# Retention, folded down phases, first round and mixer side work in another order

## The chip, the cores and the metric

The kernel runs on one core of one Trainium2 chip. The metric is the device time of one execution in microseconds (us). Engines are named as in the profile: PE is TensorE, DVE is VectorE, ACT is ScalarE, POOL is GpSimd, and SP issues the loads.

## What is computed

Two transformer-like blocks follow each other, each of two layers, on 256 tokens of 1024 features, all in float32. The first block also carries 256 context tokens.

```python
for l in range(DEPTH):                      # first block
    x = half_ffn(x, m_lat, 0)               # t + 0.5*gate*swiglu(modulate(rmsnorm(t)))
    ctx = half_ffn(ctx, m_ctx, 0)
    h_lat, h_ctx = modulate(rmsnorm(x)), modulate(rmsnorm(ctx))
    if mixer == 0: y_lat, y_ctx = fourier_layer(h_lat, h_ctx, four_w, four_b)
    else: y_lat, y_ctx = retention_layer(h_lat, h_ctx, w_in, w_out, decay, cos, sin, False)
    x = x + m_lat[5] * y_lat
    x = half_ffn(x, m_lat, 2)
for l in range(DEPTH):                      # second block
    x = x + 0.5 * swiglu(rmsnorm(x), ffn1_w_in[l], ffn1_w_out[l])
    hq, hf, hi, hg, aq, ak, av, ga, gb = split(rmsnorm(x) @ w_in[l])
    y_a = (rms(hgrn2_chunk_scan(q, 1 - f, v, log f)) * norm * silu(hg)) @ w_branch_a[l]
    y_b = dilated_window_attention(rope(rms(aq)), rope(rms(ak)), av) @ w_branch_b[l]
    x = x + (sigmoid(ga) * y_a + sigmoid(gb) * y_b) @ w_out[l]
    x = x + 0.5 * swiglu(rmsnorm(x), ffn2_w_in[l], ffn2_w_out[l])
```

The retention layer has four heads. For each head it projects q, k, v and g, turns q and k by a rope, forms scores with a decay mask in both directions, multiplies them with v, normalises the result over its 512 values, multiplies it with silu(g), and projects the four heads together through w_out.

## The kernel before, in words

**Units and rounds.** Every matrix product is a phase. A phase goes through its weight in units of 128 output columns, and four units, one for each of four slots, make a round. A slot owns a raw weight buffer, a part of `whi_all` and `wlo_all`, and one PSUM bank (0 to 3). Banks 4 to 7 serve all side work. SP loads a unit's weights of `ks` blocks (128x128 each) into `raw`. ACT casts them to the high part (`split_hi`, L1073), DVE subtracts to get the low part (`split_lo`, L1343), and both signal SP and PE. PE multiplies each block three times, whi by hi, whi by lo and wlo by hi (`block_mm`, L613 to L615). Where only 256 tokens are left, whi meets hi and lo side by side in one matmul of 512 columns, and wlo one of 256 (L608, L609, L611: the folded form). When the unit is done (`mm_done`), ACT or DVE take its result, and ACT and DVE split the slot's next weights, which then wait three slots for PE. All engines hold their own instruction list, written in the order in which the Python code issues it; between engines there are only semaphores. What stands earlier on an engine must be done earlier.

**`linear`** writes a phase for PE. It has a special first round where the input is not complete yet. With `across`, the first half of the blocks goes block by block over all four slots; without it, slot 0 waits block by block and slots 1 to 3 follow whole. `do_first` and `do_norm` make the first normalised input: root of the mean square, then eight chunks of which DVE writes `t_full` (L1518), ACT the high and DVE the low part (`xn_two`, L1507). In the very first norm, a weight split stands behind chunks 1, 3 and 5.

**Feed-forward.** `gu` phases make gate and up, POOL writes the product in two parts (`h_two`, L1930 and L1932), and a `dn` phase reads them, in two halves of 12 and 10 blocks. The first unit of the `dn` phase comes to the last block when POOL has hardly written it.

**Retention, head by head.** `ret_qk`, `ret_v`, the turning of the values (L829, read from `r_vf`, which ACT copies out), `ret_g`, the scores (L838), the masked scores `r_p` (DVE, L1647), the result (L844), ten matmuls that compute nothing (`fill`, L721), the turning of the normalised result `r_yn` (L852, after DVE's statistics and ACT's root), and DVE's product with the gate (`r_z`, L1667), which POOL splits into `z_two` (L1939, L1941). After four heads `ret_out` reads `z_two`.

**Mixer.** `mixer_order` lists the units of eight phases, and behind each unit side work that all engines read from the same list. Unit 16 is the first of `att_qk` (QK), 40 of `hi` (HI), 60 of `hg` (HG). The scan over tokens works in eight levels of four units each: `decay` behind the first unit and `totals` behind the second (DVE, L1782 to L1801), `pairs` and `keep` for half 0 behind the third and for half 1 behind the fourth. `pairs` are PE's pair scores (L996, banks 4 and 5), `keep` is DVE's copy_predicated into `g_a` (L1809). A bank of `pairs` can be written again when the copy before has read it. `rope` i turns two heads' q (i below 6) or k on DVE (L1719 to L1724); for k, PE first spreads the roots (`spread`, L894) into bank 6, which it shares with `turn`, the turning of values (L935) that ACT copies out (`w_f`, L1279). `hsum` are row sums in bank 7 (L889), `hroot` ACT's and DVE's root of them, `hspread` j its spread (L894) and product (L1823).

```python
        for i, u in enumerate((21, 25, 29, 31, 33, 37, 43, 49, 51, 53, 55, 57)):
            if i >= 6:
                put(u, "spread", i)
            put(u, "rope", i)
```

Of the kernel before, what the change touches and what calls it, by code (L numbers as in the profile page):

```python
# [23 lines left out]
P = 128  # L24
# [54 lines left out]
def build(nc, A, out, stop=None):  # L79
# [105 lines left out]
    def mixer_order():  # L185
# [76 lines left out]
    with ExitStack() as ctx:  # L262
# [337 lines left out]
        def _(pe):  # L600
# [29 lines left out]
            def linear(name, moving, T, ready=None, across=False):  # L630
# [3 lines left out]
                ks, start = ph["ks"], 0  # L634
# [3 lines left out]
                def one(it, first=False):  # L638
# [14 lines left out]
                    for s in range(SLOTS):  # L653
# [5 lines left out]
                        for k in range(ks):  # L659
                            if first and name == "ret_out" and s < 2:  # L660
                                pe.wait_ge(*ready(8 * s + k))
                            elif first and s == 0:
# [106 lines left out]
            def do_ffn(a):  # L769
                two = h2_two if a["mod"] is None else h_two  # L770
                moving, ready = normed(a["norm"], folded(a))
                for half in range(2):
                    linear(f"{a['tag']}gu{half}", moving, a["T"], ready if half == 0 else None,
                           a["T"] == 2 * SEQ and a["norm"]["n"] > 0)
                    q0 = gu_rounds(a["f"], half)
                    linear(f"{a['tag']}dn{half}", pair(two, a["T"], folded(a)), a["T"],
                           lambda k: [(h_done[k % 2], q0 + k // 2 + 2)])
# [34 lines left out]
            def do_retention(a):  # L812
                _, ready = normed(a["norm"])
                for h in range(RH):
                    def tok(s):
                        return SEQ if s < 2 else 512
                    linear(f"ret_qk{h}", lambda s, k: pair(xn_two, tok(s))(s, k), tok,
                           ready if h == 0 else None, True)
                    linear(f"ret_v{h}", pair(xn_two, 512), 512)

                    pe.wait_ge(rt["vf"], 4 * (h + 1))
                    for t in range(4):
                        if h:
                            if t < 2:
                                pe.wait_ge(rt["yn"], 2 * h)
                            else:
                                pe.wait_ge(rt["z"], 2 * h)
# [3 lines left out]
                    linear(f"ret_g{h}", pair(xn_two, SEQ), SEQ)  # L831

                    pe.wait_ge(rt["qk"], 2 * (h + 1))
# [7 lines left out]
                    pe.wait_ge(rt["p"], 4 * (h + 1))  # L841
                    for i in range(2):
                        for j in range(4):
                            mm = pe.matmul(bank[4 + i][:], r_p[:, j, i * P:(i + 1) * P], r_v[:, j, :],  # L844
# [1136 lines left out]
```

## Time and profile before

| what | value |
|---|---|
| median of three runs | 3415.88 us (3411.71 to 3420.25) |
| the profiled execution | 3413.48 us |
| its span, first to last instruction | 3411.7 us |
| granted TensorE clock, mean | 0.993 of 2.4 GHz |
| PE busy | 3312.6 us |
| DVE, ACT, POOL busy | 2301.8, 1275.3, 648.5 us |
| mean DMA rate | 149 GB/s |

The rows of the views name engine, source line, operation and what is written from what. Behind a group or an instruction, in brackets or behind the bar, stands the engine's idle time before it and whose work ended it. The granted clock is given as a share of 2.4 GHz, so 0.50 is 1.2 GHz.

### The profile page before, as it was taken

The numbers are of one execution on the slowest core, as the hardware profiler recorded it, in microseconds if no ns is written. First come the engines' busy times: TensorE is split into PE (matmuls) and PEld (weight loads), VectorE is DVE, ScalarE is ACT, GpSimd is POOL, SyncE is SP. The second block draws the span as 40 slices with busy tenths as digits, with TensorE's granted clock in tenths as the row PEclk, the third lists the DMA queues.
The fourth block names the chain that finished last, engine by engine and source line by source line (L and its number), as shares of the span: only waits on it lengthen the run. The fifth ranks groups of instructions, "written<-read, shape, count | busy, mean of one in ns | idle before, by whom it ended". The sixth has DMA issues, their size and how long they took to land.

```text
span 3411.7 us, 49602 instructions
## 1 busy us (share of the span) xinstructions
PE 3312.6 (97%) x19035; PEld 2879.9 (84%) x19035; DVE 2301.8 (67%) x2888; ACT 1275.3 (37%) x1702; POOL 648.5 (19%) x535
## 2 busy tenths in 40 slices
PE   7999999999999999999999999999999999999999
PEld 4888888888888888878888899999888889899887
DVE  3877857878686545447677657756767666765766
ACT  2322133212321233334445343365534444346443
POOL 2212322212220220003242220000323230000222
PEclk9999999999999999999999999999999999999999
DMA  5655514646364423335665653345665655333664
GB/s 195 203 162 169 154 54 146 191 145 191 111 190 150 119 73 105 93 99 158 188 175 170 174 162 112 112 121 153 180 179 163 188 165 148 111 118 108 185 190 142
DMA packets 862983, 507.68 MB, mean 149 GB/s; under 512 B 15060, under 2 KB 843024, under 8 KB 862800
## 3 DMA queue, kind: packets, MB, share of 16 engines
q1 hardware_dynamic: 862432, 503.74, 49.9%
q8 instruction: 130, 2.13, 0.2%
q0 software_dynamic: 368, 1.38, 0.1%
q14 instruction: 53, 0.43, 0.0%
HBM read 504.01 MB, written 1.05 MB: 148 GB/s over the span
## 4 chain that ended last, share of the span: by engine, by line
PE 87%; DVE 7%; ACT 3%; issue 2%; POOL 1%; SPq 0%; DMA 0%; POOLq 0%; DVEq 0%; ACTq 0%
PE bank L613 17%; PE bank L611 17%; PE bank L615 16%; PE bank L614 16%; PE bank L609 10%; PE bank L608 2%; DVE wlo_all L1343 1%; ACT whi_all L1073 1%; PE bank L996 1%; DVE t_full L1518 1%; PE bank L702 1%; PE bank L844 1%; PE bank L734 1%; POOL h_two L1932 1%; PE bank L894 0%
## 5 line engine op out<-in xcount | busy, mean ns | idle before, releaser
L1343 DVE TENSOR_TENSOR wlo_all<-raw,whi_all 128x1024 fp32r<-128x1024 f32 (+3 forms) x768 | 1018.5, 1328 | 664.1 <-ACT whi_all L1073 661.3
L1073 ACT CAST whi_all<-raw 128x1024 fp32r<-128x1024 f32 (+3 forms) x768 | 834.5, 1089 | 901.2 <-PE bank L615 565.3
L613 PE MATMUL bank<-xn_two,whi_all 128*128 128x256 f32 (+1 forms) x2848 | 971.9, 341 | 12.3 <-DVE xn_two L1507 9.2
L614 PE MATMUL bank<-xn_two,whi_all 128*128 128x256 f32 (+1 forms) x2848 | 948.0, 333 | 0.0
L615 PE MATMUL bank<-xn_two,wlo_all 128*128 128x256 f32 (+1 forms) x2848 | 947.7, 333 | 0.0
L613 PEld LDWEIGHTS bank<-xn_two,whi_all 128*128 128x128 f32 x2848 | 543.6, 191 | 70.5 <-DVE xn_two L1507 11.1
L615 PEld LDWEIGHTS bank<-xn_two,wlo_all 128*128 128x128 f32 x2848 | 542.7, 191 | 52.0
L614 PEld LDWEIGHTS bank<-xn_two,whi_all 128*128 128x128 f32 x2848 | 543.5, 191 | 50.3
L611 PE MATMUL bank<-xn_two,whi_all 128*128 128x512 f32 x1540 | 550.3, 396 | 0.0
L609 PE MATMUL bank<-xn_two,wlo_all 128*128 128x256 f32 x1760 | 459.5, 281 | 3.3 <-DVE xn_two L1507 0.9
L1930 POOL CAST h_two<-silu_g 128x256 f32 (+1 forms) x176 | 197.2, 1121 | 1392.7 <-DVE silu_g L1558 783.7
L609 PEld LDWEIGHTS bank<-xn_two,wlo_all 128*128 128x128 f32 x1760 | 331.7, 188 | 33.5 <-DVE xn_two L1504 11.1
L611 PEld LDWEIGHTS bank<-xn_two,whi_all 128*128 128x128 f32 x1540 | 289.2, 188 | 58.1
L611 PE MATMUL bank<-h_two,whi_all 128*128 128x512 f32 x800 | 284.7, 396 | 0.0
L609 PE MATMUL bank<-h_two,wlo_all 128*128 128x256 f32 x880 | 234.0, 281 | 10.1 <-POOL h_two L1932 10.1
L1932 POOL TENSOR_TENSOR h_two<-silu_g,h_two 128x256 f32 (+1 forms) x176 | 224.6, 1276 | 32.5 <-POOL h_two L1930 32.5
L613 PE MATMUL bank<-h_two,whi_all 128*128 128x512 f32 x528 | 206.2, 390 | 0.0
L615 PE MATMUL bank<-h_two,wlo_all 128*128 128x512 f32 x528 | 205.5, 389 | 0.0
L614 PE MATMUL bank<-h_two,whi_all 128*128 128x512 f32 x528 | 205.5, 389 | 0.0
L1353 DVE SCALAR_TENSOR_TENSOR ada_acc<-ada_w,sil_c,ada_acc 128x1024 f32<-128x1024 f32 x112 | 183.0, 1634 | 0.8
L609 PEld LDWEIGHTS bank<-h_two,wlo_all 128*128 128x128 f32 x880 | 165.9, 188 | 20.5 <-POOL h_two L1932 13.3
L1907 POOL TENSOR_TENSOR sumsq<-x 128x256 f32<-128x256 f32 (+1 forms) x12 | 13.0, 1087 | 874.0 <-DVE x L1530 794.5
(281 smaller groups left out, 3855.4 us busy)
## 6 DMA issues: line engine op xcount, KB each, us to landing
raw<-in_ffn_w_in SPq DMA_DIRECT2D x176, 512.0 KB, 3.8
raw<-in_w_in SPq DMA_DIRECT2D x168, 512.0 KB, 3.7
ada_w<-in_ada_w SPq DMA_DIRECT2D x128, 512.0 KB, 3.8
raw<-in_ffn_w_gate SPq DMA_DIRECT2D x88, 512.0 KB, 3.7
raw<-in_ffn_w_up SPq DMA_DIRECT2D x88, 512.0 KB, 3.8
raw<-in_ffn_w_down SPq DMA_DIRECT2D x32, 768.0 KB, 5.1
raw<-in_ret_w_in SPq DMA_DIRECT2D x48, 512.0 KB, 3.8
raw<-in_ffn_w_out SPq DMA_DIRECT2D x32, 768.0 KB, 5.1
```

The lines of the kernel that those rows point to most:

```text
L608: pe.matmul(both, whi[s][:, k, :], two, start=True, stop=False)
L609: mm = pe.matmul(o, wlo[s][:, k, :], hi, start=False, stop=False)
L611: mm = pe.matmul(both, whi[s][:, k, :], two, start=False, stop=(k == ks - 1))
L613: pe.matmul(o, whi[s][:, k, :], hi, start=(k == 0), stop=False)
L614: pe.matmul(o, whi[s][:, k, :], lo, start=False, stop=False)
L615: return pe.matmul(o, wlo[s][:, k, :], hi, start=False, stop=(k == ks - 1))
L702: mm = pe.matmul(bank[half][0:4, :], first_cs[:, j, k, :], ada_first[DC * j + k][:, half * 512:(half + 1) * 512], start=(j == 0 and k == 0 ...
L1073: act.copy(whi[s][:, 0:ks, :], raw[s][:, 0:ks, :]).then_inc(hi_done[s], 1)
L1343: tt(wlo[s][:, 0:ks, :], raw[s][:, 0:ks, :], whi[s][:, 0:ks, :].bitcast(F32), ALU.subtract).then_inc(lo_done[s], 1)
L1353: stt(ada_acc[0][:], w[:], sil_c[:, k, 0:1], ada_acc[0][:], ALU.mult, ALU.add).then_inc(ada_sum, 1)
L1930: pool.tensor_copy(hi[:, ds(2 * it + p, 1), 0:T], full).then_inc(h_rounded[p], 1)
L1932: tt(lo[:, ds(2 * it + p, 1), 0:T], full, hi[:, ds(2 * it + p, 1), 0:T].bitcast(F32), ALU.subtract).then_inc(h_done[p], 1)
```

## The change

Four places get another order. The amount of work stays the same, but for forty filling matmuls that go.

1. **First round.** ACT and DVE split the weights of all four slots before they take the root, and none between the chunks. ACT squares its chunk ahead of that. The first round is written `across`.
2. **Down phases on 256 tokens** (`last_late`): in the first round, slots 0 and 1 do all blocks but the last; then PE waits for the last block and does it for both.
3. **Retention.** The values are turned behind the first unit of `ret_g`, the scores come behind the third; the result of a head is turned behind the first unit of the next head's `ret_qk`, or of `ret_out` for the last head. `fill(10)` is gone. `ret_out` takes its first round in the slot order 0, 2, 1, 3. DVE's pieces move along through `behind`.
4. **Mixer.** The twelve ropes get other units; `hsum`, `hroot` and `hspread` come one unit later.

```diff
-        for i, u in enumerate((21, 25, 29, 31, 33, 37, 43, 49, 51, 53, 55, 57)):
+        for i, u in enumerate((23, 27, 31, 35, 39, 43, 47, 50, 51, 54, 55, 58)):
...
-        put(HG, "hsum", 0)
-        put(HG, "hroot", 0)
+        put(HG + 1, "hsum", 0)
+        put(HG + 1, "hroot", 0)
         for j in range(4):
-            put(HG + 2 + j, "hspread", j)
+            put(HG + 3 + j, "hspread", j)
...
+                    if first and last_late:
+                        for s in range(2):
+                            slot_ready(s, r)
+                            for k in range(ks - 1):
+                                if s == 0:
+                                    for w in ready(k):
+                                        pe.wait_ge(*w)
+                                block_mm(s, k, ks, tokens(s), *moving(s, k))
+                        for w in ready(ks - 1):
+                            pe.wait_ge(*w)
+                        for s in range(2):
+                            block_mm(s, ks - 1, ks, tokens(s), *moving(s, ks - 1)).then_inc(mm_done[s], 1)
...
-                           a["T"] == 2 * SEQ and a["norm"]["n"] > 0)
+                           a["T"] == 2 * SEQ)
...
-                    fill(10)
...
+                for h in range(RH):
...
+                        for s in range(SLOTS):
+                            slot_mm(f"ret_qk{h}", 0, s, pair(xn_two, tok(s)), tok(s))
+                            if s == 0:
+                                turn_result(h - 1)
+                    linear(f"ret_v{h}", pair(xn_two, 512), 512)
+                    for s in range(SLOTS):
+                        slot_mm(f"ret_g{h}", 0, s, short, SEQ)
+                        if s == 0:
+                            turn_values(h)
+                        if s == 2:
+                            scores(h)
...
+                for s in (0, 2, 1, 3):
+                    slot_mm("ret_out", 0, s, halves[s % 2], SEQ, lambda k: (rt["zlo"], (8 * (s % 2) + k) // 4 + 1))
+                    if s == 0:
+                        turn_result(RH - 1)
...
             def do_first(a):
-                split_hi(0, 0, DC)
+                take_squares(a)
+                for s in range(SLOTS):
+                    split_hi(s, 0, DC)
                 take_root(a)
...
             def do_first(a):
-                split_lo(0, 0, DC)
+                for s in range(SLOTS):
+                    split_lo(s, 0, DC)
                 take_root(a)
```

DVE in the very first norm, from the first weight split on. Before:

```order
L1343 TENSOR_TENSOR wlo_all_50<-raw0,whi_all_49 128x1024
L1482 RECIPROCAL rstd<-rstd 128x4
L1389 TENSOR_TENSOR mod<-bank5,vec 128x16 x2
L1393 SCALAR_TENSOR_TENSOR mod<-mod,vec 128x16
L1518 SCALAR_TENSOR_TENSOR t_full_56<-x_53,mod,bank7 128x256 x4
L1507 SCALAR_TENSOR_TENSOR xn_two_54<-t_full_56,mod,xn_two_54 128x256 x2
L1343 TENSOR_TENSOR wlo_all_50<-raw1,whi_all_49 128x1024
```

and now:

```order
L1384 TENSOR_TENSOR wlo_all_50<-raw0,whi_all_49 128x1024
L1384 TENSOR_TENSOR wlo_all_50<-raw1,whi_all_49 128x1024
L1384 TENSOR_TENSOR wlo_all_50<-raw2,whi_all_49 128x1024
L1384 TENSOR_TENSOR wlo_all_50<-raw3,whi_all_49 128x1024
L1526 RECIPROCAL rstd<-rstd 128x4
L1430 TENSOR_TENSOR mod<-bank5,vec 128x16 x2
L1434 SCALAR_TENSOR_TENSOR mod<-mod,vec 128x16
L1562 SCALAR_TENSOR_TENSOR t_full_56<-x_53,mod,bank7 128x256 x4
```

The splits of slots 1 to 3 moved from between the chunks to ahead of the root's reciprocal.

PE at the turn from one head to the next. L838 are the scores, L844 (now L885) the result, L721 the filling matmuls, L852 (now L859) the turning. Before:

```order
L613 MATMUL bank<-xn_two,whi_all 128x256
L614 MATMUL bank<-xn_two,whi_all 128x256
L615 MATMUL bank<-xn_two,wlo_all 128x256
L838 MATMUL bank<-r_q,r_k 128x256 x8
L844 MATMUL bank<-r_v,r_p 128x512 x8
L721 MATMUL bank<-ident 128x128 x10
L852 MATMUL bank<-ident,r_yn 128x128 x8
L613 MATMUL bank<-xn_two,whi_all 128x256
```

and now, at the result, and 24 matmuls of the next head later at the turning:

```order
L613 MATMUL bank<-xn_two,whi_all 128x256
L614 MATMUL bank<-xn_two,whi_all 128x256
L615 MATMUL bank<-xn_two,wlo_all 128x256
L885 MATMUL bank<-r_v,r_p 128x512 x8
L613 MATMUL bank<-xn_two,whi_all 128x256
```

```order
L613 MATMUL bank<-xn_two,whi_all 128x256
L614 MATMUL bank<-xn_two,whi_all 128x256
L615 MATMUL bank<-xn_two,wlo_all 128x256
L859 MATMUL bank<-ident,r_yn 128x128 x8
L613 MATMUL bank<-xn_two,whi_all 128x256
```

The scores went one unit up, the turning one unit down, and nothing is left between result and next unit.

DVE in a mixer level (the fourth of eight), from the end of its totals to its last copy. L1719 to L1724 (now L1767 to L1772) are a rope, L1809 (now L1857) the kept pairs. Before:

```order
L1699 RECIPROCAL square<-square 128x24
L1719 TENSOR_TENSOR a_s_116<-a_qk_114,rope2_119 64x512 x2
L1722 TENSOR_TENSOR a_qk_114<-a_qk_114,rope2_119 128x512
L1724 TENSOR_TENSOR a_qk_114<-a_qk_114,a_s_116 128x512
L1343 TENSOR_TENSOR wlo_all_50<-raw2,whi_all_49 128x1024
L1809 COPY_PREDICATED g_a0_110<-hmask_120,bank4 128x2x2x128
L1809 COPY_PREDICATED g_a1_111<-hmask_120,bank5 128x2x2x128
L1343 TENSOR_TENSOR wlo_all_50<-raw3,whi_all_49 128x1024
L1809 COPY_PREDICATED g_a2_112<-hmask_120,bank4 128x2x2x128
L1809 COPY_PREDICATED g_a3_113<-hmask_120,bank5 128x2x2x128
```

and now:

```order
L1747 RECIPROCAL square<-square 128x24
L1384 TENSOR_TENSOR wlo_all_50<-raw2,whi_all_49 128x1024
L1857 COPY_PREDICATED g_a0_110<-hmask_120,bank4 128x2x2x128
L1857 COPY_PREDICATED g_a1_111<-hmask_120,bank5 128x2x2x128
L1384 TENSOR_TENSOR wlo_all_50<-raw3,whi_all_49 128x1024
L1857 COPY_PREDICATED g_a2_112<-hmask_120,bank4 128x2x2x128
L1857 COPY_PREDICATED g_a3_113<-hmask_120,bank5 128x2x2x128
L1767 TENSOR_TENSOR a_s_116<-a_qk_114,rope2_119 64x512 x2
L1770 TENSOR_TENSOR a_qk_114<-a_qk_114,rope2_119 128x512
L1772 TENSOR_TENSOR a_qk_114<-a_qk_114,a_s_116 128x512
```

The rope went from ahead of the level's copies to behind them.

## Rows read from the trace of the kernel before

**Rows 1.** The page: busy time of the engines, and the ended-last chain by engine.

```profile
PE 3312.6 (97%) x19035; PEld 2879.9 (84%) x19035; DVE 2301.8 (67%) x2888; ACT 1275.3 (37%) x1702; POOL 648.5 (19%) x535
...
PE 87%; DVE 7%; ACT 3%; issue 2%; POOL 1%; SPq 0%; DMA 0%; POOLq 0%; DVEq 0%; ACTq 0%
```

**Rows 2.** Who waited for whom, PE: total us, times, longest us.

```profile
PE bank L996 <- DVE g_a L1809: 20.7, 14, 2.1
PE bank L609 <- POOL h_two L1932: 10.1, 10, 1.7
...
PE bank L852 <- DVE r_yn L1660: 3.7, 4, 0.9
PE bank L894 <- ACT w_f L1279: 3.6, 2, 1.8
PE bank L889 <- ACT w_f L1279: 3.2, 2, 1.6
PE bank L894 <- DVE g_d L1823: 2.9, 2, 1.4
PE bank L829 <- ACT r_vf L1198: 2.7, 4, 0.7
...
PE bank L844 <- DVE r_p L1647: 2.4, 4, 0.6
```

**Rows 3.** Timeline, first round, PE and ACT: start, us, instruction, idle before.

```profile
51.66 0.47 PE L613 MATMUL bank<-xn_two,whi_all 128*128 128x512 f32 x1 [1.35 <-DVE xn_two L1507]
...
70.33 0.39 PE L613 MATMUL bank<-xn_two,whi_all 128*128 128x512 f32 x1
...
83.93 0.39 PE L613 MATMUL bank<-xn_two,whi_all 128*128 128x512 f32 x1
...
86.17 1.05 ACT L1073 CAST whi_all<-raw 128x1024 fp32r<-128x1024 f32 x1 [3.91 <-PE bank L615]
```

**Rows 4.** Windows, 56 to 69 us: busy of each engine, PEclk, DMA share, GB/s.

```profile
56.00:69.00 13.00, 8.64 (x18) 5.08 (x18) 10.17 (x22) 7.17 (x12) 0.00 (x0) 0.50 0.31 92
```

**Rows 5.** Timeline of DVE, two chunks of the first norm.

```profile
54.18 0.87 DVE L1507 SCALAR_TENSOR_TENSOR xn_two<-t_full,mod,xn_two 128x256 fp32r<-128x256 f32 x2
...
55.76 0.87 DVE L1507 SCALAR_TENSOR_TENSOR xn_two<-t_full,mod,xn_two 128x256 fp32r<-128x256 f32 x2
```

**Rows 6.** Windows, 43 to 44 us, and ACT's root.

```profile
43.00:44.00 1.00, 1.00 (x10) 1.00 (x10) 0.00 (x0) 0.00 (x0) 0.00 (x0) 1.00 0.80 214
...
44.89 0.26 ACT L1105 ACTIVATE rstd<-bank,eps 128x4 f32<-128x4 f32 x1 [4.42 <-PE bank L734]
```

**Rows 7.** Timeline of retention: end of head 0, PE; end of head 3, DVE, POOL.

```profile
1323.84 7.13 PE L844 MATMUL bank<-r_v,r_p 128*128 128x512 f32 x16 [0.61 <-DVE r_p L1647]
1330.81 2.40 PE L721 MATMUL bank<-ident 128*128 128x128 f32 x20
1334.14 1.09 PE L852 MATMUL bank<-ident,r_yn 128*128 128x128 f32 x8 [0.93 <-DVE r_yn L1660]
...
1539.02 1.29 DVE L1667 TENSOR_TENSOR r_z<-bank,r_g 128x512 f32<-128x512 f32 x2 [0.85 <-PE bank L852]
...
1540.38 1.04 POOL L1939 CAST z_two<-r_z 128x1024 fp32r<-128x1024 f32 x1 [64.38 <-DVE r_z L1667]
1541.50 2.40 POOL L1941 TENSOR_TENSOR z_two<-r_z,z_two 128x1024 fp32r<-128x1024 f32 x1
```

**Rows 8.** Timeline of PE, first unit of a second down phase.

```profile
1755.57 0.39 PE L609 MATMUL bank<-h_two,wlo_all 128*128 128x256 f32 x1 [1.66 <-POOL h_two L1932]
```

**Rows 9.** Timeline of DVE, mixer of layer 0: a copy and a rope.

```profile
2116.34 0.73 DVE L1809 COPY_PREDICATED g_a<-hmask,bank 128x512 f32<-128x512 int32 x1 [0.79 <-PE bank L996]
2117.09 1.40 DVE L1719 TENSOR_TENSOR a_s<-a_qk,rope 64x512 f32<-64x512 f32 x2
2118.53 0.69 DVE L1722 TENSOR_TENSOR a_qk<-a_qk,rope 128x512 f32<-128x512 f32 x1
2119.26 0.69 DVE L1724 TENSOR_TENSOR a_qk<-a_qk,a_s 128x512 f32<-128x512 f32 x1
```

**Rows 10.** Windows, two levels of the mixer of layer 1, second half to second half.

```profile
2899.39:2918.51 19.12, 17.05 (x143) 16.83 (x143) 14.72 (x18) 7.93 (x14) 0.00 (x0) 1.00 0.38 111
2918.51:2939.00 20.49, 18.59 (x137) 18.08 (x137) 17.37 (x21) 6.37 (x12) 0.00 (x0) 0.92 0.35 103
```

More of the change, by code:

```diff
@@ L628, in ada_reduce, with slot_mm, linear @@
                     mm.then_inc(ada_cols, 1)
-            def linear(name, moving, T, ready=None, across=False):
+            def slot_mm(name, it, s, moving, T, ready=None):
                 ph = phases[name]
-                ks, start = ph["ks"], 0
+                slot_ready(s, it + ph["first"])
+                for k in range(ph["ks"]):
+                    if ready is not None:
+                        pe.wait_ge(*ready(k))
+                    mm = block_mm(s, k, ph["ks"], T, *moving(s, k))
+                mm.then_inc(mm_done[s], 1)
+            def linear(name, moving, T, ready=None, across=False, last_late=False, start=0):
+                ph = phases[name]
+                ks = ph["ks"]
                 tokens = T if callable(T) else (lambda s: T)
@@ L652, in one @@
                         return
-                    for s in range(SLOTS):
+                    if first and last_late:
[10 more added lines that the diff above has]
+                            block_mm(s, ks - 1, ks, tokens(s), *moving(s, ks - 1)).then_inc(mm_done[s], 1)
+                    for s in range(2 if first and last_late else 0, SLOTS):
                         slot_ready(s, r)
@@ L813, in do_retention, with turn_values @@
                 _, ready = normed(a["norm"])
[L814 to L819, printed above, removed]
+                def turn_values(h):
                     pe.wait_ge(rt["vf"], 4 * (h + 1))
@@ L830, in do_retention, with scores @@
                         mm.then_inc(rt["vt"], 1)
-                    linear(f"ret_g{h}", pair(xn_two, SEQ), SEQ)
+                def scores(h):
                     pe.wait_ge(rt["qk"], 2 * (h + 1))
@@ L840, in do_retention, with turn_result @@
                         mm.then_inc(rt["s"], 1)
[L841 to L844, printed above, removed]
-                                           start=(j == 0), stop=(j == 3))
-                        mm.then_inc(rt["y"], 1)
-                    fill(10)
+                def turn_result(h):
                     pe.wait_ge(rt["yn"], 2 * (h + 1))
@@ L1117, in do_norm @@
                 if a["n"]:
+                    take_squares(a)
                     take_root(a)
@@ L1415, in body @@
                             split_lo(s, r + 1, ahead)
+                        if behind is not None:
+                            behind(it, s)
                         if ends and SLOTS * r + s in ends:
@@ L1604, in do_retention, with take_result @@
                 cos, sin = rope1[:, 0, :], rope1[:, 1, :]
+                def take_result(h):
+                    g3 = phases[f"ret_g{h}"]["first"] + 2
+                    for s in range(SLOTS):
+                        dve.wait_ge(bank_free[s], g3)
+                    for b in range(2):
+                        dve.wait_ge(rt["yt"], 2 * h + b + 1)
+                        tt(r_z[:, 2 * b:2 * b + 2, :], bank[6 + b][:].rearrange("p (e t) -> p e t", e=2),
+                           r_g[:, 2 * b:2 * b + 2, :], ALU.mult).then_inc(rt["z"], 1)
                 for h in range(RH):
@@ L1629, in rope @@
                         tt(dst[:, 1, 0:SEQ], r_t[:, 2, :], r_t[:, 3, :], ALU.add).then_inc(rt["qk"], 1)
-                    stream(f"ret_qk{h}", rope, True)
+                    stream(f"ret_qk{h}", rope, True, behind=lambda it, s: h and s == 0 and take_result(h - 1))
                     dve.wait_ge(rt["expo"], h + 1)
@@ L1661, in do_retention @@
                             ALU.mult).then_inc(rt["yn"], 1)
-                    g3 = phases[f"ret_g{h}"]["first"] + 2
-                    for s in range(SLOTS):
-                        dve.wait_ge(bank_free[s], g3)
-                    for b in range(2):
-                        dve.wait_ge(rt["yt"], 2 * h + b + 1)
-                        tt(r_z[:, 2 * b:2 * b + 2, :], bank[6 + b][:].rearrange("p (e t) -> p e t", e=2),
-                           r_g[:, 2 * b:2 * b + 2, :], ALU.mult).then_inc(rt["z"], 1)
                 def add(it, s, r):
```

57 lines of the change are left out of this document (33 added, 24 removed).

## The prediction

> **What bounds the kernel now.** I read the page first. TensorE (PE) is busy 3312.6 us of a span of 3411.7 us, and it makes 87% of the chain that ended last [rows 1]; no weight load is waited for after the first 50 us. So the sum is made on PE alone: a change can only take away PE's idle time, PE's slow time, or matmuls that compute nothing. Anything another engine does is hidden until PE waits for it. The second view, who waited for whom on PE, prices the idle time [rows 2]. The third, the timeline and the windows around each wait, tells what is behind it, and how fast PE's clock was. PE's matmuls of 512 columns follow each other every 0.2267 us in steady work (60 of them from 70.33 to 83.93 us) [rows 3]; I use 0.227 us for 512 columns and half of it for 256.
>
> **The change part by part.**
>
> *First round.* The first round of linear work starts at 51.66 us, and its fourth slot is done when ACT takes it at 86.17 us [rows 3]: 34.5 us for 96 matmuls that need 96 x 0.2267 = 21.8 us. Two things cost the rest. DVE and ACT put a weight split between every two normalised chunks, so the last chunk comes only at 66.9 us, while slots 1 to 3 wait behind slot 0; and in the 13 us from 56 to 69 the granted clock is 0.50, the lower level of 1.2 GHz, after PE was mostly idle [rows 4]. The change does the four splits before the norm and lets all slots use a chunk as it comes. A chunk then costs DVE two pieces of 0.79 us, 1.58 us in all (54.18 to 55.76 us) [rows 5], while its 12 matmuls take PE 12 x 0.2267 = 2.72 us. PE is slower than its supplier, so it starts at about the same 51.7 us and never stops: end at 51.7 + 21.8 = 73.4 us, **12.8 us** earlier. The cost is that ACT and DVE now wait for three more weight blocks ahead of the root. The loads run until about 44 us (the DMA share is still 0.80 from 43 to 44), and ACT takes the root at 44.89 us [rows 6]. The last cast is then done by about 45, a table load and the root follow, and the reciprocal ends some 0.3 us after PE wants it. I take 12.5 us. Bounds: 6 us, if the clock still falls for 13 us with PE busy (half of 13), and 12.8 us.
>
> *Retention, four heads.* Now PE waits 2.7 us (4 times) for the values to be evacuated before it turns them and 2.4 us (4) for the scores [rows 2]. With one or two slots of the gate phase in between (24 matmuls x 0.113 = 2.7 us each) both waits are covered: **5.1 us**. Behind the result matmuls stand ten filling matmuls, in 20 records, that take from 1330.81 to about 1333.2, and a wait of 0.93 us; from 1330.97, the end of the results, it is 3.17 us until the turning starts at 1334.14 [rows 7]. The first slot of the next head, 2.9 us with its overlap, comes in that place, so 0.3 us stays: 2.9 us x 3 = **8.6 us** for three heads. For the fourth the cover is a slot of the output phase, 2.8 us. There the turned result is late next: DVE has to finish slot 0's residual and split first, then multiplies (1.29 us), and POOL needs 1.04 + 2.40 us for its two pieces [rows 7]. The result reaches z_lo some 6.2 us after the turning; slot 2 and half of slot 1 cover 4.2 us. PE waits 2.0 us where it now waits 0.4. The fourth head gives 3.17 - 0.4 - 1.6 = 1.2 us. Sum **14.9 us**; bounds 10 (each head's turn waits 1 us more) and 17.
>
> *Down phases.* Ten times PE stops before the last block of the first slot until POOL has written it, 10.1 us in all [rows 2], one of 1.66 us in each second half [rows 8] and so about 0.36 us in each first. Now slot 1's blocks but the last go ahead of it: at least nine blocks of 768 columns, 9 x 0.34 = 3.1 us, more than any wait. The first slot is free later by that much, but the next use of it comes two slots (7 us) on, and its residual and splits need about 5. **10.1 us**; bounds 8 and 10.1.
>
> *Mixer, two layers.* DVE decides when a level's second half of pair scores can start: it needs the first copy_predicated. A rope of four instructions, 1.40 + 0.69 + 0.69 with gaps, is 2.77 us (2117.09 to about 2119.86) [rows 9], and before it stands between the totals and that copy. It now stands behind the level's last copy. From a level's last copy to the next level's first, DVE has the rope 2.8, three splits 3.4, decays 2.3, totals 2.4 and the copy 0.7 = 11.6 us. By the time these have to be done PE has run from one second half to the next, 17.05 us [rows 10], less about 4.3 us from its start to the end of DVE's last copy (ACT's pieces 1.8, a split 1.14, two copies of 0.62 to 0.73 as in rows 9): 12.8 us. That leaves 1.2 us free. So the five waits of 1.30 to 2.07 us of a layer, 9.1 of 10.35 us, go, and those of 0.97 us (a reciprocal stands there) and 0.28 us stay: 2 x 9.1 = **18.2 us**. The row sums one unit later clear the copies of ACT: 2 x 1.6 = **3.2 us** [rows 2]. The third key spread no longer comes right behind turned values, 2 x 1.82 us [rows 2], but two key ropes are now in neighbouring units just before a turn that shares their bank; DVE is then some 0.9 us late for it: **1.8 us** net. The wait of 1.44 us a layer for the spreads of the hg root (L894 for g_d) [rows 2] is set by ACT's work of one fixed unit; it moves from the fourth spread to the third and stays. Sum of mixer waits **23.2 us**; bounds 15 (the pairing costs 4 us a layer) and 27.
>
> **Sum** 12.5 + 14.9 + 10.1 + 23.2 + 10.8 = **71.5 us**. The profiled execution took 3413.48 us with a span of 3411.7, 2.4 us under the median of 3415.88. From itself it gives 3342.0; I forecast the median, 3415.9 - 71.5 = **3344 us**, 2.1% less.
>
> The Trainium skill speaks against one part. "TensorE: Matmul & The Clock Gate", section "HAM oscillation", says that pauses between bursts throttle the array again and cost half of the throttled time. By that rule the filling matmuls that the change drops did a job, and the result would be the second rival's 3352 us rather than 3344; that half of the time is lost agrees with the 1.54 us of rows 10.
>
> **The rivals.**
> 1. *The clock's share does not come.* The lower level is granted at norms too, where no such wait stands, so the waits may not be what brings it. If the seven stay, the time is 3344 + 11 = 3355; if the first round also falls to it for its 13 us, 3361. For it: layer 1 has a wait of 1.94 without a low stretch. Against: no level behind a short wait has one. Chance 0.14.
> 2. *The head turns lose the clock.* Without the filling matmuls, the idle 0.3 to 2 us of four turns and the output phase bring one low stretch each: 5 x 1.54 = 8 us, 3352. Chance 0.08.
> 3. *DVE becomes the bound in the mixer.* If the 1.2 us of slack is not there (a POOL operation beside it, ropes in neighbouring units), each of 14 levels still waits 1 us, and the low clock with it: 3344 + 14 + 7 = 3365. For it: DVE is busy 17.37 of 20.49 us in a level with a second piece [rows 10]. Chance 0.08.
> 4. *It does less than it says in the down phases or the first round*, because another engine was late as well: half of 22.6 us, 3355. Chance 0.06.
> 5. *Slower than before.* The fills and the ordered waits keep TensorE at the upper level, and without them retention and the mixers run at 1.2 GHz for long. PE-bound work at the lower level loses half of its time, so 71.5 us are lost again when it lasts 143 us; over the four heads of 68 us it would be +136 us, 3480. The rows 4 show 13 us of it after a gappy stretch, never more. Chance 0.02.
>
> **How the numbers follow.** The forecast has 0.62. Rivals 1 to 4 have 0.36 together and lie between 3352 and 3365. The forecast's own bounds are about 3331 (the three low places at norms go too, the last head does not wait, the mixer gives 27) and 3358. The range is 3330 to 3363: it leaves out the end of rival 3, rival 5, and gains beyond the upper bounds. A measurement of this kernel tells about 0.3% (10 us) from no change. Only rival 5 is on the other side, and for within 0.3% most terms would have to fail at once: faster 0.97, same 0.01, slower 0.02.
>
> **What would show it.** In the profile after: the first round's fourth slot taken at about 73.7 us with clock 1.00 throughout; no wait of PE for h_two; no filling matmuls and no waits for r_vf and r_p in retention, about 0.3 us for r_yn three times, about 2 us for z_two once; PE's wait for g_a under 3 us in total instead of 20.7, none behind row sums, one of about 1.5 us for g_d in each layer; levels of 17 us at clock 1.00. PE's busy time should fall by about 9 us of fills, 11 us of slow clock and what the first round's slow matmuls were worth. Wrong would be: a wait for g_a near 14 us, low clock in levels without a wait, or a new wait for weights (wlo_all) after the paired key ropes.

## The result and the profile after

| | before | after |
|---|---|---|
| median, us | 3416.98 (4 runs, 3411.71 to 3420.25) | 3336.19 (4 runs, 3335.01 to 3337.18) |
| ratio | | 0.9765, 95% from 0.9748 to 0.9782 |
| profiled execution, us | 3413.48 | 3336.21 |
| its span, us | 3411.7 | 3334.4 |

The changed kernel is 2.35% faster. The forecast was 3344 us, the range 3330 to 3363: the time lies in the range, 8 us below the forecast. The gain is 79.7 us against the median of 3415.88 shown above, 80.8 us against that of four runs, and 77.3 us between the two profiled spans. The forecast gain was 71.5. The sums below are made on the two traces, so against 77.3.

The page of after, busy time and the chain by engine (before: [rows 1]):

```profile
PE 3281.3 (98%) x18955; PEld 2859.5 (86%) x18955; DVE 2294.6 (69%) x2888; ACT 1274.4 (38%) x1702; POOL 648.4 (19%) x535
...
PE 92%; DVE 4%; ACT 2%; issue 1%; SPq 0%; DMA 0%; POOL 0%; DVEq 0%; ACTq 0%
```

The 80 matmul records that are missing (19035 to 18955) are the forty filling matmuls, two records each. PE's idle time fell from 99.1 to 53.1 us, its busy time from 3312.6 to 3281.3. Who waited for whom on PE, after (line, total us, times, longest us; before: [rows 2]):

```profile
PE bank L1034 <- DVE g_a L1857: 3.1, 4, 1.3
PE bank L932 <- DVE g_d L1871: 2.9, 2, 1.4
...
PE bank L609 <- POOL z_two L1989: 1.5, 1, 1.5
PE bank L973 <- issue: 1.4, 2, 0.7
...
PE bank L859 <- DVE r_yn L1715: 1.3, 4, 0.4
```

L1034 is L996 of before: its wait for the kept pairs went from 20.7 us (14 times) to 3.1 (4). The waits for h_two, r_vf, r_p and both for w_f have no row any more. The wait for g_d is unchanged at 2.9, that for z_two grew from 0.4 to 1.5, and that at L973 (`turn`, the turning of values, L935 before) is new. The timeline of after, at the places that the prediction named (start, us, instruction, idle before):

```profile
44.16 1.04 ACT L1111 CAST whi_all<-raw 128x1024 fp32r<-128x1024 f32 x1 [1.87 <-DMA raw<-in_ffn_w_up]
46.52 0.26 ACT L1147 ACTIVATE rstd<-bank,eps 128x4 f32<-128x4 f32 x1
...
52.46 0.47 PE L613 MATMUL bank<-xn_two,whi_all 128*128 128x512 f32 x1 [1.35 <-DVE xn_two L1551]
74.54 1.05 ACT L1111 CAST whi_all<-raw 128x1024 fp32r<-128x1024 f32 x1 [1.19 <-PE bank L615]
1320.99 1.09 PE L859 MATMUL bank<-ident,r_yn 128*128 128x128 f32 x8 [0.30 <-DVE r_yn L1715]
1511.08 1.09 PE L859 MATMUL bank<-ident,r_yn 128*128 128x128 f32 x8 [0.39 <-DVE r_yn L1715]
1517.91 0.39 PE L609 MATMUL bank<-z_two,wlo_all 128*128 128x256 f32 x1 [1.54 <-POOL z_two L1989]
```

The first round runs from 52.46 to 74.54, 22.1 us instead of 34.5 [rows 3]. Windows of after: the stretch of [rows 4], then two levels of layer 0's mixer from one second half to the next (before, in layer 1: [rows 10]), then most of each mixer, then retention (bounds, length, busy us of PE, PEld, DVE, ACT, POOL, granted clock, DMA share, GB/s):

```profile
56.00:69.00 13.00, 13.00 (x59) 10.78 (x58) 7.54 (x18) 6.35 (x11) 0.00 (x0) 1.00 0.01 1
...
2056.55:2073.37 16.82, 16.82 (x145) 16.77 (x144) 14.67 (x17) 8.03 (x14) 0.00 (x0) 1.00 0.43 125
2090.13:2106.90 16.77, 16.77 (x138) 16.56 (x137) 14.58 (x16) 6.37 (x12) 0.00 (x0) 1.00 0.43 126
2000.00:2300.00 300.00, 294.41 (x2361) 289.00 (x2361) 211.13 (x264) 152.04 (x254) 0.00 (x0) 1.00 0.42 123
2780.00:3080.00 300.00, 294.42 (x2361) 289.00 (x2360) 210.78 (x263) 151.51 (x253) 0.00 (x0) 1.00 0.43 124
1240.00:1560.00 320.00, 314.65 (x1747) 265.86 (x1746) 179.42 (x288) 123.22 (x167) 34.57 (x26) 1.00 0.37 108
```

Levels of 19 to 20.5 us became levels of 16.8 us in which PE never stops, and both mixers run at clock 1.00. Layer 1's mixer before, taken for 300 us from 45 us behind its start (42 in after), had 2216 matmuls instead of 2361, at clock 0.98:

```profile
2840.00:3140.00 300.00, 282.90 (x2216) 276.22 (x2215) 202.59 (x250) 142.32 (x235) 0.00 (x0) 0.98 0.40 117
```

The first matmul that sums the squares of a norm (L754, L734 before) marks the stages. Four of its rows in after:

```profile
419.30 0.35 PE L754 MATMUL bank<-ones,sumsq 128*128 128x1 f32 x2 [0.42 <-ACT silu_g L1142]
1247.96 0.35 PE L754 MATMUL bank<-ones,sumsq 128*128 128x1 f32 x2 [0.42 <-ACT silu_g L1142]
1557.60 0.35 PE L754 MATMUL bank<-ones,sumsq 128*128 128x1 f32 x2 [0.74 <-ACT silu_g L1142]
1955.79 0.35 PE L754 MATMUL bank<-ones,sumsq 128*128 128x1 f32 x2 [0.65 <-ACT silu_g L1142]
```

Before they stood at 430.93, 1258.41, 1586.41 and 1988.26. A stage is the time from one of these markers to the next. With the other markers, the 77.3 us by which the span is shorter are made of:

| part | forecast, us | traces, us |
|---|---|---|
| start and first round | 12.5 | 11.6 (0.8 later start, 12.4 shorter) |
| from the first round to retention (419 to 1248) | 0 | -1.2 (the clock at the norms) |
| retention | 14.9 | 18.4 |
| down phases | 10.1 | 11.1 (3.7 + 5.0 + 2.5) |
| mixers and their clock | 23.2 + 10.8 | 37.4 (19.5 + 17.9) |
| sum | 71.5 | 77.3 |

### The profile page after: what moved, and what is told of

The parts are those of the page before. It is cut to its first block, busy times and chain, and to the rows that moved or that the text cites. A ratio compares the mean times of both kernels' runs of the same rounds, so it can differ in the third digit from the quotient of the medians.

```text
span 3334.4 us, 49439 instructions
## 1 busy us (share of the span) xinstructions
PE 3281.3 (98%) x18955; PEld 2859.5 (86%) x18955; DVE 2294.6 (69%) x2888; ACT 1274.4 (38%) x1702; POOL 648.4 (19%) x535
## 4 chain that ended last, share of the span: by engine, by line
PE 92%; DVE 4%; ACT 2%; issue 1%; SPq 0%; DMA 0%; POOL 0%; DVEq 0%; ACTq 0%
PE bank L613 18%; PE bank L611 18%; PE bank L615 18%; PE bank L614 18%; PE bank L609 10%; PE bank L608 2%; PE bank L1034 1%; DVE t_full L1562 1%; PE bank L722 1%; PE bank L885 1%; ACT whi_all L1111 1%; PE bank L754 1%; DVE wlo_all L1384 1%; PE bank L932 0%; PE bank L927 0%
## 5 line engine op out<-in xcount | busy, mean ns | idle before, releaser
L609 PEld LDWEIGHTS bank<-xn_two,wlo_all 128*128 128x128 f32 x1760 | 331.9, 189 | 33.2 <-DVE xn_two L1548 10.8
L611 PEld LDWEIGHTS bank<-h_two,whi_all 128*128 128x128 f32 x800 | 150.3, 188 | 32.8
```

Source lines behind the costliest of these rows:

```text
L609: mm = pe.matmul(o, wlo[s][:, k, :], hi, start=False, stop=False)
L611: mm = pe.matmul(both, whi[s][:, k, :], two, start=False, stop=(k == ks - 1))
```

## The experiments

**1 to 4. Each part undone alone.** In `undo_mixer` the two tables of the mixer are as before:

```
-for i, u in enumerate((23, 27, 31, 35, 39, 43, 47, 50, 51, 54, 55, 58)):
+for i, u in enumerate((21, 25, 29, 31, 33, 37, 43, 49, 51, 53, 55, 57)):
-put(HG + 1, "hsum", 0); put(HG + 1, "hroot", 0); put(HG + 3 + j, "hspread", j)
+put(HG, "hsum", 0); put(HG, "hroot", 0); put(HG + 2 + j, "hspread", j)
```

> The changed kernel with the mixer's side work in the old order; all else as changed. By the forecast's terms it loses 23.2 us of waits and 10.8 us of slow clock: 3336.2 + 34.0 = 3370. If every stop of PE costs about 0.2 us more than its recorded idle time (the restart of the matmul stream), 16 stops a time for both layers add 3 us: 3373. PE's wait for g_a is 20.7 us again and seven levels have a clock of 0.92. If the low clock depends on where PE stands and not on the waits, the number of such levels differs from seven, 1.54 us each.

Measured 3373.70 us (3373.01 to 3374.83), ratio 0.9877 [0.9861, 0.9894]: 37.5 us more than the change. Its waits, and a stretch of layer 1's mixer:

```profile
PE bank L1034 <- DVE g_a L1857: 20.7, 14, 2.1
...
PE bank L932 <- ACT w_f L1320: 3.6, 2, 1.8
PE bank L927 <- ACT w_f L1320: 3.2, 2, 1.6
PE bank L932 <- DVE g_d L1871: 2.9, 2, 1.4
```

```profile
2840.00:2930.00 90.00, 82.20 (x621) 80.92 (x620) 65.37 (x74) 28.83 (x52) 0.00 (x0) 0.92 0.36 105
```

All the waits of before are back, with nothing else of the change undone. The low clock is back too, in six places (a low place is one stretch at the lower level), though not the same ones: one in layer 0 and five in layer 1, where before had four and three. That gives the price of both by themselves. In the old order the stage of layer 0's mixer took 415.78 us with four low places (before) and 410.94 with one (`undo_mixer`), that of layer 1 414.16 with three and 417.48 with five. So a low place costs 1.6 to 1.7 us, and without any the two stages would take 409.3 and 409.2, which is 25.9 us more in all than the 396.29 each of after. That is the price of the waits; the other 11.4 of the 37.4 us are the clock's.

`undo_down` gives the first slot of the down phases its last block in its own turn again:

```
-..., last_late=folded(a))
+...)
```

> The changed kernel with slot 0 of the folded down phases waiting for its last block as before. Recorded idle alone: 10.1 us in ten waits, 3336.2 + 10.1 = 3346.3. Idle plus a restart of about 0.2 us each: 3348.6. If the two traces' difference of 12.4 us in these stages came from elsewhere, it is under 3345.

Measured 3347.63 us (3346.80 to 3349.69), ratio 0.9802 [0.9785, 0.9818]: 11.4 us more. One row is new against after:

```profile
PE bank L609 <- POOL h_two L1980: 10.1, 10, 1.7
```

Ten waits that the profile puts at 10.1 us cost 11.4 by the median. The stages of the two traces tell more: where neither has a low place, a stage with two down phases takes 196.11, 195.46 and 195.47 us instead of 193.62, 192.97 and 192.99. That is 2.49, 2.49 and 2.48 us for two waits that are recorded with 2.02 to 2.05, or 0.21 to 0.23 us a stop beyond its record.

`undo_first` puts the splits of slots 1 to 3 back between the chunks and lets slots 1 to 3 wait behind slot 0:

```
-for s in range(SLOTS):
-    split_hi(s, 0, DC)
+split_hi(0, 0, DC)
...
+if a["n"] == 0 and k in (1, 3, 5):
+    split_hi((k + 1) // 2, 0, DC)
...
-... a["T"] == 2 * SEQ)
+... a["T"] == 2 * SEQ and a["norm"]["n"] > 0)
```

(and the same for `split_lo` on DVE).

> The changed kernel with the first round as before (one split ahead, three between the chunks, slots 1 to 3 behind slot 0). Forecast's term: 3336.2 + 12.5 = 3348.7, with a clock of 0.50 for about 13 us. If half of the gain was the clock's alone and the clock stays up this time, about 3342.

Measured 3347.91 us (3347.02 to 3348.33), ratio 0.9801: 11.7 us more. The stretch of [rows 4] is again at the lower level of 1.2 GHz:

```profile
56.00:69.00 13.00, 8.79 (x18) 5.19 (x19) 9.94 (x21) 6.93 (x12) 0.00 (x0) 0.50 0.31 93
```

`undo_ret` has PE's and DVE's retention of before: the values are turned right behind the value phase, the scores are made behind the whole gate phase, ten filling matmuls stand behind the result, and it is turned before the next head. In words, the edit is:

```
-scores(h) in the gate phase's slot 2, turn_values(h) in its slot 0
-turn_result(h - 1) behind the next head's first slot
+turn_values(h) ahead of the gate phase, scores(h) behind all of it
+fill(10); turn_result(h) at the head's end
```

> The changed kernel with the whole retention layer in the old order, filling matmuls included. Forecast's term: 3336.2 + 14.9 = 3351.1. With a restart of about 0.2 us for each of eight to twelve stops: 3353. The rival that the fills held the clock up: it would gain clock back and be under 3349.

Measured 3354.25 us (3353.33 to 3354.74), ratio 0.9819 [0.9803, 0.9836]: 18.1 us more.

The four prices are 37.5, 11.4, 11.7 and 18.1, in sum 78.7 of the 79.7 to 80.8 us of the whole change. Within some 2 us the parts add up: none hides another's gain. And each agrees with its stages of the two traces within 0.5 us. The kernels were not all run together, and before, which was run beside each group of them, had medians of 3415.4 to 3418.0: a difference of 2 us between two kernels may come from that.

**5 and 6. Which half of the first round's change matters.** `first_across` takes only the early splits away (the first two hunks of `undo_first`) and keeps the slots going chunk by chunk:

> The changed kernel, but with the weight splits of slots 1 to 3 between the chunks again; the first round still goes over all slots block by block. Slot 3's weights are ready only behind the sixth chunk (about 64 us), so PE cannot pass the first block before: 93 matmuls x 0.227 = 21 us from there, 85 us, and some slow clock behind the long stop. 3336.2 + 11 to 14 = 3347 to 3350, nothing of the 11.7 us that undoing both cost. The rival, that going over all slots gives most by itself: under 3342.

Measured 3348.70 us (3347.86 to 3349.99), ratio 0.98 [0.9784, 0.9817]: 12.5 us more than the change, so the order of the slots alone gains nothing. PE, which now wants the other slots' weights with the first chunk, waits for the splits between the chunks:

```profile
58.81 0.80 PE L613 MATMUL bank<-xn_two,whi_all 128*128 128x512 f32 x1 [4.13 <-DVE wlo_all L1385]
...
63.91 0.80 PE L613 MATMUL bank<-xn_two,whi_all 128*128 128x512 f32 x1 [3.45 <-DVE wlo_all L1385]
```

`first_splits` keeps the early splits and lets slots 1 to 3 wait behind slot 0 (the last hunk of `undo_first`):

> The changed kernel, all four splits ahead of the root, but slots 1 to 3 wait behind slot 0 in the first round. Slot 0 ends with the last chunk at about 63.5 us, then 72 matmuls x 0.227 = 16.3 us: 79.8 instead of 74.4, so 3336.2 + 5.5 = 3341.7. Slow clock while PE has only 3 matmuls per 1.58 us adds up to 3 us when it lasts into slot 1: 3342 to 3345.

Measured 3341.70 us (3340.61 to 3342.75), ratio 0.9779 [0.9763, 0.9796]: 5.5 us more. Here PE stops in each chunk, since DVE needs 1.58 us for one and a single slot gives PE only three matmuls. The timeline of PE and ACT, and a window:

```profile
53.52 0.50 PE L613 MATMUL bank<-xn_two,whi_all 128*128 128x512 f32 x1 [0.55 <-DVE xn_two L1551]
...
55.10 0.50 PE L613 MATMUL bank<-xn_two,whi_all 128*128 128x512 f32 x1 [0.61 <-DVE xn_two L1551]
...
56.67 0.50 PE L613 MATMUL bank<-xn_two,whi_all 128*128 128x512 f32 x1 [0.61 <-DVE xn_two L1551]
...
79.51 1.05 ACT L1111 CAST whi_all<-raw 128x1024 fp32r<-128x1024 f32 x1 [3.91 <-PE bank L615]
```

```profile
52.00:68.00 16.00, 12.36 (x47) 8.23 (x48) 11.36 (x27) 8.26 (x15) 0.00 (x0) 1.00 0.03 8
```

The fourth slot is taken at 79.51 instead of 74.54. In this execution the clock stays at 1.00 with a stop in every chunk, where it was 0.50 with the splits in between. Two of the four executions took 2.1 us longer at a mean clock of 0.996 instead of 0.998; where they lost it is not on record. So the early splits alone are worth 11.7 - 5.5 = 6.2 us, the lower level among them, and the slots going across another 5.5, but only on top of the early splits.

**7. Were the filling matmuls needed for the clock?** `fills_back` puts ten of them behind each head's result, in the new order:

```
                         mm.then_inc(rt["y"], 1)
+                    fill(10)
```

> The changed kernel with the ten filling matmuls of each head put back behind the result, ahead of the next head's first slot. Forecast's accounting: 4 x 2.24 us more, less the 0.3 us waits for r_yn with their restarts, about 4 x 0.4: + 7.3, 3343.5. The rival, that fills hold TensorE's clock up: some clock comes back and the time is at 3340 or less.

Measured 3344.50 us (3343.01 to 3347.37), ratio 0.9785 [0.9769, 0.9802]: 8.3 us more. In its waits there is no r_yn any more and z_two is later:

```profile
PE bank L609 <- POOL z_two L1990: 2.1, 1, 2.1
```

The fills cost about their own length (20 records, one every 0.112 us, so 4 x 2.24 us), less the 1.3 us of waits for r_yn that they cover, plus 0.6 at z_two. Retention is at clock 1.00 without them (the 1240 to 1560 row of after above) and no faster with them:

```profile
1240.00:1560.00 320.00, 316.11 (x1771) 268.55 (x1770) 173.30 (x278) 120.24 (x162) 30.50 (x21) 0.99 0.35 102
```

The 0.99 is one low place right behind the longer wait for z_two, at 1526.9 us; from 1240 to 1520 the clock is 1.00 here too. The rival that the head turns lose the clock falls.

**8. The key ropes by themselves.** `keys_old` puts the key ropes from the second on where they were and leaves the first, the query ropes and the row sums changed:

```
-... 43, 47, 50, 51, 54, 55, 58)
+... 43, 47, 49, 51, 53, 55, 57)
```

> The changed kernel with the key ropes from the second on in their old units (49, 51, 53, 55, 57); q ropes, first key rope and row sums as changed. Per layer the wait of 1.82 us for turned values comes back and the one of 0.71 us at a turn goes, each with its restart: + 1.1 us, 3336.2 + 2.2 = 3338.4. If ropes in neighbouring units cost DVE more than that, it is faster than the changed kernel. Low clock behind the 1.8 us wait would add 1.5 us each.

Measured 3340.36 us (3336.96 to 3342.12), ratio 0.9773 [0.9757, 0.979]: 4.2 us more, 2 more than the traces' waits allow. Those are as foreseen: the third key spread waits again, and L973 does not.

```profile
PE bank L932 <- ACT w_f L1320: 3.6, 2, 1.8
```

That is 3.6 less 1.4, 2.2 us, and the two mixer stages of the trace are 2.5 us longer together (397.55 and 397.52 for 396.29 each). The rest lies outside the mixers, where the edit changes nothing. The same stretch at a norm, up to which the two programs are the same, first in this kernel, then in the change:

```profile
500.00:510.00 10.00, 8.83 (x48) 8.78 (x49) 4.60 (x11) 2.65 (x7) 0.00 (x0) 0.66 0.18 53
```

```profile
500.00:510.00 10.00, 8.77 (x56) 8.34 (x56) 6.55 (x16) 3.65 (x10) 0.00 (x0) 0.83 0.18 53
```

At a norm, where PE works with pauses of up to 1.2 us, the lower level is granted for more or less of the time from one execution to the next. Such a place costs 0.6 to 1.6 us: the stage behind this norm took 373.1 us in the traces without one (before, `first_splits`), 373.7 to 374.7 with one (after, `more_mixer`) and 375.2 to 375.5 with one twice as long (`keys_old`, `more_both`, `fills_back`); the retention stage of after took 309.64 without one, and the same work 310.6 with one (`undo_down`, `undo_first`), where PE's next wait for DVE is 0.3 us or less instead of 0.85. So edits worth 2 us can't be priced by the median alone; a stage without such a place in either trace can price them.

**9. One query rope one place early.** `one_early` moves the fifth query rope ahead of its level's copies again:

```
-(23, 27, 31, 35, 39, 43, ...
+(23, 27, 31, 35, 37, 43, ...
```

> The changed kernel with one rope of each mixer (the fifth) back in its old unit 37, ahead of the copies of level 5; everything else as changed. DVE as the cause: PE waits once more per layer, for g_a, 1.0 to 1.9 us with 0.2 us of restart: 2.4 to 4.2 us in all, 3339 to 3340. If such a wait alone brings the lower clock, 1.5 us each on top: 3341.5 to 3343.5. If ropes are not the cause, 3336.

Measured 3342.34 us (3340.66 to 3343.52), ratio 0.9787 [0.9772, 0.9802]: 6.1 us more. One wait of some 2 us is back in each layer:

```profile
PE bank L1034 <- DVE g_a L1857: 6.7, 6, 2.1
```

Around it, with the waits at 2107.84 in layer 0 and at 2893.79 in layer 1:

```profile
2090.00:2112.00 22.00, 19.90 (x147) 19.40 (x147) 19.80 (x23) 6.98 (x13) 0.00 (x0) 0.92 0.41 120
2876.00:2898.00 22.00, 19.90 (x162) 19.46 (x161) 19.66 (x23) 6.93 (x13) 0.00 (x0) 1.00 0.41 120
```

The same wait brings the lower level in one layer and not in the other. The recorded waits are 3.6 us. The two mixer stages are 3.69 and 2.07 us longer than in after: 1.8 recorded and some 0.2 for the stop in each, and 1.6 for the low place in the first. That is 5.8 of the 6.1.

**10 to 12. The waits that the change leaves.** `more_mixer` moves, in each layer, one root a unit later, the last five key ropes one unit earlier each (one of them three), and the spreads of the hg root:

```
-put(QK + c + 2, "root", c // 12)
+put(QK + c + 2 + c // 23, "root", c // 12)
-... 43, 47, 50, 51, 54, 55, 58)
+... 43, 47, 49, 50, 51, 54, 57)
-put(HG + 3 + j, "hspread", j)
+put(HG + (2, 3, 4, 6)[j], "hspread", j)
```

> The changed kernel with three more moves in the mixer: key ropes at 47, 49, 50, 51, 54, 57; the second root of the row sums one unit later, behind the kept pairs; the spreads of the hg root at 62, 63, 64, 66. Per layer the 0.71 us wait at a turn, the 1.25 us wait for g_a and 1 us of the 1.44 us wait for g_d should go, 0.2 us of restart with the first two: 3.4 us, 3336.2 - 6.7 = 3329.5. If DVE's backlog from three ropes in a row only moves the waits: 3335 to 3338.

Measured 3329.29 us (3327.56 to 3329.82), ratio 0.9746 [0.9732, 0.9759]: 6.9 us less than the change. The two mixer stages are 4.1 us shorter each (392.17 and 392.20), 8.2 in all; the norms of this execution have more of the low clock than those of after. The waits for g_d and at L973 are gone, and of the 3.1 us for g_a this is left:

```profile
PE bank L1034 <- DVE g_a L1857: 0.6, 2, 0.3
```

`more_ret` turns a head's result one slot later, and at the end lets both slots of the first half of the tokens go before the blocks of the second half, four blocks of each at a time:

```
-if s == 0:
+if s == 1:
     turn_result(h - 1)
...
-for s in (0, 2, 1, 3): slot_mm("ret_out", ...)
+for s in (0, 2): slot_mm("ret_out", ...)
+for k0 in (0, 4):
+    for s in (1, 3):
+        pe.wait_ge(rt["zlo"], 3 + k0 // 4)
+        for k in range(k0, k0 + 4): block_mm(s, k, ...)
```

> The changed kernel with the turning of a head's result behind the second slot of the next head instead of the first, and ret_out's first round doing the first four blocks of slots 1 and 3 before it needs the last head. Three waits of 0.3 us and one of 1.54 go, with restarts: 1.5 + 1.7 = 3.2 us, 3333.0. If the later z stops ACT or POOL: 3336 or more.

Measured 3334.08 us (3333.69 to 3335.14), ratio 0.9762 [0.9749, 0.9775]: 2.1 us less. z_two's wait is 0.2 instead of 1.5, r_yn's 0.4 instead of 1.3, which is 2.2 us; the retention stage, with no low place in either trace, is 2.95 us shorter (306.69 for 309.64), near the 3.2 expected:

```profile
PE bank L859 <- DVE r_yn L1724: 0.4, 1, 0.4
...
PE bank L609 <- POOL z_two L1998: 0.2, 1, 0.2
```

`more_both` has both edits.

> Both sets of further moves together: 3336.2 - 6.7 - 3.2 = 3326.3 if they add up.

Measured 3326.76 us (3325.93 to 3326.87), ratio 0.9739 [0.9726, 0.9753]: 9.4 us less than the change, the best version. Its page:

```profile
PE 3279.8 (99%) x18955; PEld 2860.7 (86%) x18955; DVE 2287.0 (69%) x2888; ACT 1274.1 (38%) x1702; POOL 650.1 (20%) x535
```

PE is idle for 44 us of 3324.1, most of it at the start and the norms.

## Why the prediction was right, and where it was off

**The bound and the method** held. PE set the end in both kernels, and each wait that was to go is gone. DVE didn't become the bound (rival 3): the levels shown above have no idle time of PE. The clock's share came, and with the waits put back it was lost again (rival 1), retention without fills stayed at 1.00 (rival 2), and the down phases and the first round gave what they were to give (rival 4). The long stretch at 1.2 GHz of rival 5 did not appear. Two sums of the prediction don't come out as written: the bounds named for the low end (15 for the clock, 17 for retention, 27 for the mixer) give 3334 rather than 3331, and rival 3's 3365 takes 7 us for places that the forecast's own term puts at 10.8. The measured time hangs on neither.

**First round.** Forecast 12.5, measured 11.6. The matmuls never stop and the clock is 1.00, as foreseen, and from start to the fourth slot taken it is 22.1 us (21.8 foreseen). The start is 0.8 us later instead of 0.3, and not for the weights: the last cast ends at 45.20, a table load of 1.28 us follows, and the root at 46.52 is still in time. In both traces the round starts 8.76 us after PE's first sum of squares, at 42.90 before and 43.70 in after. This sum is late because of PE's first work, which makes a matmul every 0.85 us up to 15.0 us before and up to 16.4 in after, and then one every 0.43:

```profile
11.33 10.57 PE L702 MATMUL bank<-ada_first,first_cs 128*4 128x512 f32 x20 [2.56 <-DMA ada_first<-in_ada_w]
11.29 11.41 PE L722 MATMUL bank<-ada_first,first_cs 128*4 128x512 f32 x20 [2.49 <-DMA ada_first<-in_ada_w]
```

Where a kernel with the same start changed pace early, at about 15.2 us, the round starts at 51.98 (`undo_mixer`), 0.3 us later than before and 5.6 behind the root. So the forecast's 0.3 was right, and the other 0.5 us belongs to this execution.

**Retention.** The waits for r_vf and r_p are gone. r_yn is 0.30 to 0.39 us, foreseen as 0.3. z_two is 1.54 us, foreseen as 2.0. One place of lower clock at a norm (near 1261 in before) is gone from this stage, by chance; the experiments put it at 1.0 us (310.6 for 309.64). Without it, the stage gave 17.4 against the 14.9 of the forecast.

**Mixers.** 0.97, here 1.25, and 0.28 stay at g_a, and 1.44 at g_d, as foreseen. The pairing of the key ropes costs 0.7 us a layer, not 0.9. All seven places of lower clock are gone; by `undo_mixer` they were worth 11.4, where the forecast had 10.8. But the norms, which the forecast left as they were, cost 1.4 us net, by chance: 1.2 more between 419 and 1248, 1.0 less in retention, and 1.2 more behind 1758, where after has a low place twice as long as before. Net, the clock gave 10.0.

**The step that was mis-sized** is in nearly all terms: a stop of PE was priced at its recorded idle time. `undo_down` shows it alone, with 2.49 us a stage for 2.02 to 2.05 recorded. Two readings show where that comes from. First, the down phase around the wait of [rows 8], the timeline of PE before:

```profile
1753.39 0.28 PE L609 MATMUL bank<-h_two,wlo_all 128*128 128x256 f32 x1
1753.51 0.40 PE L611 MATMUL bank<-h_two,whi_all 128*128 128x512 f32 x1
...
1755.79 0.40 PE L611 MATMUL bank<-h_two,whi_all 128*128 128x512 f32 x1
```

The matmul at 1753.51 would be followed after 0.23 us; the next one starts at 1755.57, 2.06 us after it. So 1.83 us are lost to its start, where the row says 1.66: the record of the last matmul runs 0.17 us past the point at which the next would begin. The one behind comes 0.22 us after instead of 0.12, another 0.1. In all 1.93 us, 0.27 more than recorded. Second, a level: before, 19.12 us with a wait of 2.07, that is 17.05 of PE work; in after, a level without a stop takes 16.82 and 16.77. That is 0.23 to 0.28 us for one stop. Some 30 stops went (10 in the down phases, 8 in retention, 12 net in the mixers), and 30 x 0.22 = 6.6 us. With it the sum closes: 71.5 + 6.6 (stops) - 0.8 (clock, 10.0 for 10.8) + 0.5 (z_two) + 0.4 (key pairs) - 0.9 (start and first round) = 77.3, as measured; that it does so to the tenth is luck, since each term is good to a few tenths. By part: down phases 10.1 + 10 x 0.22 = 12.3, which the measured 11.1 and the 1.2 behind 1758 make; retention 14.9 + 1.8 + 0.5 + 1.0 = 18.2 of 18.4; mixers 34.0 + 2.6 + 0.6 + 0.4 = 37.6 of 37.4.

The other 2.4 to 3.5 us between 77.3 and the 79.7 to 80.8 of the medians are where the profiled execution of before lay: by so much under its medians, while that of after lay on its own median.

**What the Trainium skill's page said** ("TensorE: Matmul & The Clock Gate", section "HAM oscillation"): that pauses between bursts throttle the array again; the pauses of its own case are waits of some 3 to 5 us for a transfer. The runs agree for the first round of `first_across` with its stops of 3.5 to 4 us (granted clock 0.52 from 56 to 69). In the mixers the lower level also came behind waits of 1.8 to 2.1 us, shorter than those of the section, though not behind all of them. It did not come in retention without fills, whose pauses are 0.3 to 1.5 us, nor, in the profiled execution, with stops of 0.6 us in every chunk of the first round. So the prediction read the section too widely when it took it to speak for the filling matmuls.

**Left open.** Why a wait of some 2 us brings the lower level in one layer and not in the other, and why its places at norms differ between executions of one and the same program: no run tells.

## What to carry to other kernels

Where PE is the bound and is busy 97% of the span, read its waits one by one, and price a stop from the start of the matmul before it to the start of the one behind it, less the steady distance, not by the idle time in the row. Work on another engine that isn't needed now (here a rope of 2.8 us) belongs behind that engine's next delivery to PE, even when the engine is busy only two thirds of the time. Where a neighbour that is ready can cover a pause, it takes the place of filling matmuls too: try the kernel without them.

## What the runs showed of the hardware

- A stop of PE costs 0.2 to 0.3 us beyond its recorded idle time, in streams of 256 and 512 columns: 0.21 to 0.23 by the stages of `undo_down`, 0.27 by the rows around one stop, 0.23 to 0.28 by a level of the mixer.
- A place at the lower clock costs 1.5 to 1.7 us in a mixer, and 0.6 to 1.6 at two norms, where a wait of PE for DVE behind it gets shorter. It is not fixed by the program: before has four and three of them in its two layers, the same mixers in `undo_mixer` one and five. The lower level can be granted while PE is never idle, shortly after a pause. In after, behind a wait of 1.06 us at 1758.24 and small matmuls:

```profile
1758.00:1762.00 4.00, 3.76 (x29) 3.76 (x29) 0.00 (x0) 0.19 (x1) 0.00 (x0) 0.86 0.00 0
1762.00:1766.00 4.00, 4.00 (x19) 4.00 (x20) 0.94 (x3) 0.52 (x2) 0.00 (x0) 0.50 0.00 0
```

- PE's clock stayed at the upper level with a stop of 0.6 us every 1.6 us for the 16 us shown of `first_splits` (one execution), but fell in the same place of the program with the stops of 3.5 to 4 us of `first_across`.
